# Loading the next experts' weight pieces right behind the slot table, ahead of the gathered rows of the first block

## What is computed

```python
weights = g_p * (e_p / jnp.sum(e_p, axis=-1, keepdims=True))
experts = g_idx * EXPERTS_PER_GROUP + e_idx          # two experts for each frame
...
xb = h[slot_tok].reshape(n_blocks, MOE_BLOCK, h.shape[1])     # the gathered rows

def run_block(args):
    xblk, e = args                                   # 128 rows that all go to expert e
    return (jax.nn.silu(xblk @ w_gate[e]) * (xblk @ w_up[e])) @ w_down[e]
...
y_sorted = yb[dest] * expert_w.reshape(A)[order][:, None]
return jax.ops.segment_sum(y_sorted, tok_sorted, num_segments=T).astype(h.dtype)
```

## Time and profile before

| | us |
|---|---|
| median of three runs | 1719.93 |
| lowest and highest of the three | 1717.57, 1723.35 |
| profiled execution, its time | 1721.89 |
| profiled execution, its span | 1719.2 |
| expert part in it, first gather to last scatter | 1082 to about 1680 |

### The profile page before, as it was taken

The page is one execution under the profiler, slowest core; times in us unless marked ns, Lnnn a source line. Parts: engine busy times, 40 slices in busy tenths (PEclk is TensorE's granted clock), DMA queues, the critical chain, the costliest instruction groups (busy, mean ns, idle before and its releaser), DMA issues.

```text
span 1719.2 us, 23126 instructions
## 1 busy us (share of the span) xinstructions
PE 1597.7 (93%) x8247; PEld 1304.3 (76%) x8247; DVE 1042.1 (61%) x1247; ACT 766.0 (45%) x812; POOL 565.2 (33%) x452
## 2 busy tenths in 40 slices
PE   7999999999999999995899995699999999999993
PEld 6888787778877778884688884478878787777772
DVE  5211355565655425444455555788888888888885
ACT  4310332332332332214222213477777777777773
POOL 2311354342553404320001011243344344344334
PEclk9999999999999999997899997799999999999997
DMA  6221432332230404327333333699999999999986
GB/s 220 99 92 68 127 117 77 117 96 68 62 117 31 138 35 153 117 97 274 130 110 110 129 148 151 232 366 361 362 371 369 362 375 366 370 372 373 367 297 233
DMA packets 111808, 346.39 MB, mean 201 GB/s; under 512 B 15996, under 2 KB 44844, under 8 KB 86016
## 3 DMA queue, kind: packets, MB, share of 16 engines
q1 hardware_dynamic: 101312, 327.08, 51.6%
q0 software_dynamic: 10432, 18.45, 4.1%
HBM read 301.90 MB, written 65.34 MB: 214 GB/s over the span
## 4 chain that ended last, share of the span: by engine, by line
PE 25%; DMA 13%; POOL 4%; DVE 4%; issue 4%; ACT 2%; SPq 1%; POOLq 0%; ACTq 0%
DMA x_nat<-h_mid,gather_at 6%; DMA we_raw<-in_w_experts 5%; PE banks_ffn L1777 2%; PE banks_ffn L1779 2%; PE banks_ffn L1778 2%; DVE we_lo L1939 2%; PE banks_ffn L1285 2%; PE banks_ffn L1287 2%; PE banks_ffn L1286 2%; POOL x_mid L2024 2%; PE banks_ffn L1272 2%; PE banks_ffn L1273 2%; PE banks_ffn L1274 2%; PE banks_ffn L1279 1%; PE banks_ffn L1795 1%
## 5 line engine op out<-in xcount | busy, mean ns | idle before, releaser
L1939 DVE TENSOR_TENSOR we_lo<-we_raw,we_hi 128x2048 fp32r<-128x2048 f32 x192 | 432.7, 2288 | 56.5 <-ACT we_hi L1842 53.3
L1842 ACT ACTIVATE we_hi<-we_raw 128x2048 fp32r<-128x2048 f32 x186 | 352.9, 1916 | 88.9 <-PE banks_ffn L1779 72.8
L956 PE MATMUL p_bank<-w_hi,ht_hi 128*128 128x512 f32 x720 | 305.5, 424 | 2.4 <-DVE ht_lo L723 1.6
L958 PE MATMUL p_bank<-w_hi,ht_lo 128*128 128x512 f32 x720 | 284.5, 395 | 0.0
L957 PE MATMUL p_bank<-w_lo,ht_hi 128*128 128x512 f32 x720 | 283.5, 394 | 0.0
L1777 PE MATMUL banks_ffn<-we_hi,x_hi 128*128 128x512 f32 x512 | 207.3, 405 | 2.9 <-DVE x_lo L1943 2.9
L924 POOL TENSOR_TENSOR beta<-beta,prod 128x512 f32<-128x512 f32 (+3 forms) x120 | 131.7, 1110 | 217.5 <-DVE prod L776 217.5
L1779 PE MATMUL banks_ffn<-we_hi,x_lo 128*128 128x512 f32 x512 | 201.6, 394 | 0.0
L1778 PE MATMUL banks_ffn<-we_lo,x_hi 128*128 128x512 f32 x512 | 200.8, 392 | 0.0
L776 DVE TENSOR_TENSOR_SCAN prod<-keep,prod 128x512 f32<-128x512 f32 (+3 forms) x120 | 128.8, 1103 | 83.8 <-ACT keep L631 78.7
L719 DVE COPY stage<-p_bank 128x512 f32<-128x512 f32 x90 | 61.9, 688 | 172.1 <-PE p_bank L958 171.8
(11 more groups left out here) (325 smaller groups left out, 2743.2 us busy)
## 6 DMA issues: line engine op xcount, KB each, us to landing
we_raw<-in_w_experts SPq DMA_DIRECT2D x192, 1024.0 KB, 11.0
projected<-stage SPq DMA_DIRECT2D x90, 256.0 KB, 2.0
w_raw<-in_w_main SPq DMA_DIRECT2D x80, 256.0 KB, 4.8
gates<-projected SPq DMA_DIRECT2D x9, 1024.0 KB, 4.9
qkvr<-projected SPq DMA_DIRECT2D x9, 768.0 KB, 5.6
o_nat<-mixed SPq DMA_DIRECT2D x9, 512.0 KB, 3.3
x_mid<-x_new SPq DMA_DIRECT2D x9, 512.0 KB, 2.9
h_mid<-h_new SPq DMA_DIRECT2D x9, 512.0 KB, 2.6
```

The source lines that it names most:

```text
L956: pe.matmul(out, ht_hi[:, k, rows], w_hi[:, j], start=(k == 0), stop=False)
L958: last = pe.matmul(out, ht_lo[:, k, rows], w_hi[:, j], start=False, stop=(k == KD - 1))
L1842: act.activation(w_hi[:, j], w_raw[:, j], ACT.Copy).then_inc(high[j], 1)
L1939: dve.tensor_tensor(w_lo[:, j], w_raw[:, j], w_hi[:, j].bitcast(F32), ALU.subtract).then_inc(split[j], 1)
```

## The change

The two waits are taken out. SyncE issues the eight loads right behind the load of the slot table, each as soon as its own buffer is free. Nothing else is different: no instruction is added, and the other engines' programs have the same instructions in the same order.

```diff
         sp.dma_start(table[:], io["slot_table"][0:EXPERTS * P, :]...).then_inc(table_in, 16)
 
-        sp.wait_ge(first_gathered, 16)
-        sp.wait_ge(gathered, 16)
         for b in (1, 2):
             for j in (G0, U0, G1, U1):
                 load_piece(sp, j, b, b)
```

## The result

| | kernel before | changed kernel |
|---|---|---|
| median of eight runs, us | 1721.56 | 1727.14 |
| lowest and highest, us | 1717.45, 1723.35 | 1723.81, 1729.38 |
| ratio to the kernel before | 1 | 1.0034, 95% interval 1.0023 to 1.0045 |
| span of the profiled execution, us | 1719.2 | 1725.3 |

The change makes the kernel slower by 0.34%, 5.8 us at this ratio. The interval is 4.0 to 7.7 us.

What follows compares the result with a forecast made beforehand. The expert part's start was taken to hang on the first gathered rows, with DMA later a little slower than TensorE. Gather +4.0 us, lead and clock zero: 1719.93 + 4.0 = 1723.9 us, 0.23% up; range 1718 to 1728.5.

Steps and rivals of the forecast that it cites:

- The two waits cost nothing and hold back four loads: SyncE at the experts' start: only idle time lost; block 1's four loads issue from about 1079.8, first lead 9.1 us.
- What the loads do to the first gather: Block 0's first gather meets four pieces of 1.05 MB ahead of it and lands 4.0 us later.
- the two rows that bounded it: Earlier-trace gathers beside loads without a scatter in front, from 1101 us (+1.7 us) and 1119 us (+4.0 us).
- rival A: First gather waits for the whole load backlog: +6.6 us, 1726.5 us, slower; chance 0.17.
- What the lead is worth: Block 1's earlier weight loads gain zero: block 1 waits for TensorE, and the DMA engines run dry at 1111 anyway.
- The cover: TensorE's first pass over expert 0's G0; block 1's weights could come about 3 us later before it is gone.
- The second gather is covered: `x_second`, late by the same as the first, is needed some 8 us after the first matmul; covered up to 9 us late.
- TensorE's clock: Rise from half to full speed near 1095 moves with the start: zero taken, 1.6 us put into the range.
- Everything else: Table load still ahead of the weight loads, frame numbers not later, no other engine's program changed.
- What I said would show it: Changed profile: loads issued 1079.8 to 1082, first gather 6 to 9 us, first matmul near 1094.8, DMA idle after about 1091.
- B: First gather loses less than 1 us, or its delay is taken up before block 1: 1720.5 us; chance 0.14.
- C: Expert part bound by DMA from its first load, lead kept: 9.1 us less the gather's 4.0, 1714.8 us; chance 0.08.

Runs made afterwards that it cites:

- the first wait kept: Against the kernel before, only SyncE's wait for the second gather (block 1's rows) taken out: 1720.87 us against 1720.55, ratio 1.0000 (0.9991 to 1.0009).
- the kernel without any lead: Kernel before, both waits kept, four extra 1 MB copies from weights to HBM scratch put ahead of the waits: 1731.85 us, ratio 1.0060 (1.0044 to 1.0076).
- the gather put first: Kernel before with GpSimd's loop turned round, gather for block i + 2 ahead of the scatter of block i - 2: ratio 0.9996 (0.9987 to 1.0006).

## Why the prediction was right

The forecast was 0.23% up, 4.0 us on the medians; measured are 5.6 us between the medians and 4.0 to 7.7 us by the interval. The direction, the cause and the place are those of the forecast. By its own steps:

- **The two waits cost nothing and hold back four loads.** Right: the first loads are issued from 1080.13, against the 1079.8 that I gave.
- **What the loads do to the first gather: +4.0 us.** Measured +4.6 (8.94 against 4.38). Of the two rows that bounded it I took the upper one, and the value came out a little above it. The bound itself was too low: the two gathers were issued beside two and three pieces in flight, this one beside four. That the sum came so near owes something to luck, since the rows gave a size and not the two parts of which the delay consists (2.5 us of later start, 2.0 us of slower flow). The range held it because it reached to rival A.
- **What the lead is worth: zero.** Right, and shown three times, within what a run can tell: the first wait kept is level with the kernel before, the kernel without any lead loses no more than its gather, and in the changed kernel itself the blocks take 580.68 us against 580.72. Even the lead of the loads shrank on its way: the first was issued 9.1 us earlier by the table's load, and the last of the four landed at 1095.1 instead of 1101.2, with the gathers' rows moving among them. The cover that I gave as about 3 us was 2.4: in the kernel before, block 1's G0 landed at 1093.6, 4.7 us behind its issue, and was rounded at 1096.06.
- **The second gather is covered.** Right, though it was not late by the same 4.0 us: it took 11.2 us, 5.7 more than before, and TensorE turned its rows in the middle of block 0 without a wait.
- **TensorE's clock: zero, 1.6 us in the range.** The granted clock was 0.58 in 1096 to 1100 and 1.00 from 1100, 4 us later than in the earlier trace rows, like the start itself. From the first matmul to the first rounding for block 1 it is 4.80 us (1100.54 − 1095.74), before 5.27: 0.5 us in favour.
- **Everything else.** The profiled execution shows 6.1 us of span. 4.6 are the gather and 0.4 lie ahead of the stage. The remaining 1.1 are behind the start of the last scatter's issue, where GpSimd needed 2.80 us for what took 1.59. In the changed kernel VectorE was splitting when this scatter was issued at 1676.42 (its splits ran from 1673.26 to 1679.96), in the kernel before it began to split only at 1672.16, 0.65 us behind the start of the issue: the wait of GpSimd for a running split that the experiments show. Where in a split the last scatter falls differs from kernel to kernel, and the stretch to the final gather varies between 587.7 and 589.4 us among those that leave the loop as it is, so I don't count it as an effect of the change. Whether a part of the medians' 5.6 us beyond the gather's 4.6 is the change's can't be told: the interval holds both.

What I said would show it came out, with three misses: TensorE's wait for the first rows was 9.45 us where I gave 7 to 9, the first matmul was at 1095.74 where I gave 1094.8, and the DMA engines fell idle at about 1095 and not at 1091, since the gathers' rows shared them with the loads. They stayed idle to 1104, and the later waits for gathers were 20.6 us against 18.7.

Of the rivals, **A** (the whole backlog) came closest in its number, 1726.5 us, and is still not what happens. The time could not have told the two apart, since 6.6 us and 4.6 us both lie in its interval. The trace of the changed kernel settles it: the gather's landing is 4.6 us later and not 6.6, and it landed 3.8 us ahead of a load that was issued before it. **B** and **C** fall. C deserves a word, because half of it is true: loads do set the pace of the later blocks, as the gather put first showed. What is false in it is that a lead ahead of block 0 reaches them. The buffers end it.

The Trainium skill (DMA: Bandwidth & Descriptors, section Queues, rings and completion order) says that a DMA engine takes its queues in turn, a packet at a time. The trace agrees for the time in which both queues move, 175 packets to 178 from 1087 to 1091. It shows nothing of such turns in the 3.2 us before the gather's first rows move. The size that I had worked out by taking a turn for one piece, 2.5 us, was too small: the delay is 4.6 us.

## What to carry to other kernels

A transfer that nobody waits for is not free when it is issued ahead of a small one that everybody waits for: count what is in flight when the small one starts, and hold the large ones back until it has landed, which here costs nothing. An early load only helps as far as there are free buffers behind it; look for the stretch in which the DMA engines fall idle, and ask whether the lead survives it. And a wait that looks superfluous because its result is used elsewhere may be there to keep the way free for a small transfer.

## What the runs showed of the hardware

- A gather of 128 rows of 4 KB by GpSimd's queue, beside loads of 1 MB on SyncE's, takes 4.3 us alone and 6.8 and 8.9 us with two and four pieces ahead of it. Its rows began to move 0.7 us behind the end of its issuing when alone and 3.2 us behind it with two or four loads ahead; with four, the packets of both queues then went one for one. It landed 3.8 us ahead of a load that was issued before it.
- Four copies from HBM to HBM ahead of it made it 14.2 us, in one run. They moved 33 KB a packet on the mean, the loads 7.4 KB.
- VectorE holds up what GpSimd issues. An indirect DMA took GpSimd 1.05 us to issue with VectorE idle and 2.95 to 3.00 us when a split of a weight piece was running, in four kernels; it was back at 1.05 us when the split was moved. Over all traces, 95 of the 101 gathers issued during a split were issued 0.88 to 0.93 us behind its end, and a split that began later held up none of the 289 issues that it met. The Trainium skill (DMA: Bandwidth & Descriptors, section SWDGE vs HWDGE vs iDMA) names a mechanism of this kind: GpSimd writes its descriptors into SBUF, and VectorE locks it out of there while it runs in its two-port mode. The runs show the delay and who was busy, not the lock, nor whether the splits run in that mode.
